# A hybrid decoder trunk on one core: up products of the recurrent stage as three single-pass products, merged products kept in used-up input rows, and the first weight tile loaded by quarters

## The chip, the cores and the metric

The kernel runs on one core of a Trainium2 chip. The metric is the device time of one execution in microseconds. The kernel before was run three times: 2075.19, 2076.61 and 2077.98 us, median 2076.61 us. The profile comes from one more execution of 2077.07 us.

## The reference, cut to what matters

One inference step of a decoder layer on 288 token columns: 256 of a prompt, 32 of eight short sequences. `D_MODEL` is 2048. All weights and inputs are float32.

```python
xn = rmsnorm(x, g_mix)
u  = xn @ w_in                 # columns: RWKV | mLSTM | pooling | three merge gates of 2048
o_rw   = rwkv7_mix(u_rw, ...)  # delta-rule recurrence, 16 heads x 64
o_ml   = mlstm_mix(u_ml, ...)
o_pool = pool_mix(u_pool, ...)
g = split(u_gate, 3)
merged = sigmoid(g0)*(o_rw@w_up_rwkv) + sigmoid(g1)*(o_ml@w_up_mlstm) + sigmoid(g2)*(o_pool@w_up_pool)
x = x + merged @ w_out
# then cross-attention into 256 memory tokens, a hierarchical mixture of experts, final RMSNorm
```

The change touches the input projection's first tile, the products `o_ml @ w_up_mlstm` and `o_pool @ w_up_pool` (here called the up products), and where `merged` lies.

## The kernel before, in words

All matrices are kept with features on the 128 partitions and tokens (T = 288) along the free axis. The program runs five blocks one after the other, each with its own instruction order per engine and semaphores between engines: `stage_front` (the input projection, mLSTM, pooling), `stage_rwkv` (the recurrent stage), `stage_merge`, `stage_cross`, `stage_moe`. Instructions on an engine run in the order written; `Steps` is a helper that gives each named step a semaphore count, and `q`, `v`, `a`, `g_` are those counters of TensorE, VectorE, ScalarE and GpSimd.

Most large products use split operands. A float32 tile w is rounded into `high` (by ScalarE, a copy into type fp32r), the remainder w - high is written as `rest` (by VectorE, over the raw weights), and the same is done for the activations. The product is then three fp32r matmuls: high by x_high, high by x_low, rest by x_high. In the trace these are single matmuls; a plain float32 matmul appears as two records.

**Front.** `stage_front` takes 58 tiles of 128 output columns from `w_main`, three slots deep (`weights(t)`, L303). Tile 0 waits for the activations: ScalarE makes `x_high` from 16 rows (L579), then `w_high` of tile 0 (`split`, L537); VectorE makes `x_rest` (L765), then `w_rest` (`rest`, L643); TensorE pairs high and low passes (L375, L376) and ends with the rest passes (L380). GpSimd squares and adds the 16 rows for the RMS norm meanwhile (L821 to L826).

**Recurrent stage.** `stage_rwkv` has a loop of N = 8 iterations. Each handles two heads of the recurrence, a long chain of small products and elementwise steps, and fills TensorE's waits with pieces of large products: `filler(name, lo, hi)`. The fills of an iteration are four gate tiles G00, G01, G10, G11 (16 row blocks of x, split, 48 passes each) and four up tiles U00, U01, U10, U11 (8 row blocks of `o_ml` or `o_pool`, plain float32, 8 products each, L1088). In a name the first digit is which of two output tiles, the second is 0 for mLSTM and 1 for pooling. One iteration on TensorE runs: U00, first half of U01, the small products z, a (L1120, L1121) and ss (L1123), G00, rest of U01, G01, transposes, small products; then seven levels l = 0 to 6 of a block inverse, each with products z (L1168), t (L1189) and u (L1192); fills stand between z and t and behind u: G10 at level 1, U10 at level 2 in two halves, U11 at levels 4 and 5 in quarters. Then the output part with G11 in pieces, and the group norm: products mean (L1286), bonus, var (L1290).

The edge between two iterations is a chain: var (TensorE), ve (VectorE L1561), groot (ScalarE L1372, square root), a reciprocal and three more steps on VectorE up to o (L1568), then z of the next iteration, which waits for o. ScalarE after groot runs `split("00")` (L1309), then kksq (L1318, which waits for o), then tz and ta (L1320, L1322). VectorE goes on with dx_v, us_v, half of `rest("00")` (L1420), sg (L1435), a, cs and so on to ssm, the other half of `rest("00")`, a reciprocal, kk (L1454). ScalarE does `split("01")` when G00's high passes are through, then the exponentials from kk (ek, L1327).

Before the loop ScalarE and GpSimd copy the 16 rows of `x_rest` from the place where `mrg` will lie into `ring` and `x_low_end`, since the merged products are written over it; after the loop they copy them on to `o_ml`'s place for `stage_merge` (L1299, L1375, L1580, L1610).

Of the kernel before, what the change touches and what calls it, by code (L numbers as in the profile page):

```python
# [126 lines left out]
def program(nc, A, O):  # L127
    with ExitStack() as ctx:
# [40 lines left out]
        with ExitStack() as mix:  # L169
# [5 lines left out]
            x_new = rounded("x_rest_late", [P, KD, T], "o_ml")  # L175
# [16 lines left out]
def stage_front(nc, ctx0, A, O, env):  # L192
# [9 lines left out]
    with ExitStack() as ctx:  # L202
# [29 lines left out]
        square, dn = placed("square", [P, T], "front", 10272), placed("dn", [P, T], "front", 10272)  # L232
# [13 lines left out]
        slot = [sem(f"f_slot{s}") for s in range(SLOTS)]  # L246
        squares, rooted, summed, variance, inverse = (sem(f"f_{n}") for n in "squares rooted summed var inverse".split())
# [53 lines left out]
        def _(sp):  # L301
# [61 lines left out]
        def _(pe):  # L363
            mm, ident = nc.tensor.matmul, K("ident")

            def tile(t):
                pe.wait_ge(w_high, t + 1)
# [117 lines left out]
            for t in range(O0):  # L485
# [3 lines left out]
                if t == SUM_AFTER:  # L489
                    pe.wait_ge(constants_in, 16)  # L490
                    pe.wait_ge(squares, 2 * KD - 1)
# [35 lines left out]
        def _(act):  # L527
# [48 lines left out]
            for k in range(KD):  # L576
                if k % 4 == 0:
                    act.wait_ge(x_in[k // 4], 16)
                fn(x_h[:, k, :], x[:, k, :], ACT.Copy, scale=par("g_mix", k)).then_inc(x_high, 1)  # L579
            for t in range(-1, O0):  # L580
# [57 lines left out]
        def _(dve):  # L638
# [128 lines left out]
            for t in range(SUM_AFTER + 2):  # L767
                rest(t)
            dve.wait_ge(summed, 1)
# [43 lines left out]
        def _(pool):  # L813
# [3 lines left out]
            for k in range(KD):  # L817
                if k % 4 == 0:
                    pool.wait_ge(x_in[k // 4], 16)
                if k == 0:  # L820
                    tt(rstd[:, :], x[:, k, :], x[:, k, :], ALU.mult).then_inc(squares, 1)  # L821
                    continue
                pool.wait_ge(squares, 2 * k - 1)
                tt(square[:, :], x[:, k, :], x[:, k, :], ALU.mult).then_inc(squares, 1)
                pool.wait_ge(squares, 2 * k)
                tt(rstd[:, :], rstd[:, :], square[:, :], ALU.add).then_inc(squares, 1)  # L826
# [79 lines left out]
def stage_rwkv(nc, ctx0, A, O, env):  # L906
# [11 lines left out]
    with ExitStack() as ctx:  # L918
# [21 lines left out]
        env["sb"]("x_low_end", [P, T], ctx)  # L940
# [5 lines left out]
        x_h, x_old, x_new = env["x_h"], env["x_l"], env["x_new"]  # L946
        x_l, x_le = rounded("rx_low", [P, KD - 1, T], "ring", 8192), rounded("rx_low_end", [P, T], "x_low_end")
        low = lambda k: x_l[:, k, :] if k < KD - 1 else x_le[:, :]
# [12 lines left out]
        xl_in, xl_out = sem("w_xlin"), sem("w_xlout")  # L961
# [3 lines left out]
        pe_steps = ["U00", "z", "a", "ss", "H00", "G00", "U01", "H01", "G01", "tr0", "tr1", "tr2"]  # L965
        pe_steps += [f"bk{x}{h}" for x in H for h in H] + ["sk0", "sk1", "w0", "w1"]
        fill_after = {1: ["G10"], 2: ["U10"], 5: ["U11"]}
        for l in LV:
            pe_steps += [f"z{l}"] + ([] if l == 0 else (["H10"] if l == 1 else []) + [f"t{l}", f"u{l}"] if l < 6 else [f"u{l}"])
# [6 lines left out]
        dve_steps = ["dx_v", "us_v", "sg", "a", "cs", "cen", "csc", "csm", "ssm", "l00",  # L976
                     "rec", "kk", "kap", "rt", "b", "bt", "l01", "ka", "kp", "kt", "rkk", "s00", "m00", "s01", "m01"]
        dve_steps += [f"bk{x}{h}" for x in H for h in H] + ["sk0", "sk1", "wm0", "w0", "wm1", "w1"]
        for l in LV:
            dve_steps += (["l10"] if l == 1 else []) + ([f"u{l}", f"t{l}"] if l == 0 else [f"t{l}", f"u{l}"] if l < 6 else [f"u{l}"])  # L980
            if l < 2:
                dve_steps += ["su0", "st0"] if l == 0 else ["su1"]
# [4 lines left out]
            if l == 5:  # L987
                dve_steps += ["l11"]
        dve_steps += ["s0", "s1a", "s1", "ds", "dsp", "ysum", "s11", "d", "m11", "ve", "grec", "y", "bon", "o"]
# [1901 lines left out]
```

## Time and profile before

| | us |
|---|---|
| median of 3 runs | 2076.61 |
| profiled execution | 2077.07 |
| its span | 2075.3 |
| TensorE busy in the span | 1850.8 (89%) |
| VectorE busy | 943.3 (45%) |
| ScalarE busy | 596.6 (29%) |
| GpSimd busy | 394.6 (19%) |
| recurrent stage, first up product to the last iteration's end | about 484 to 1169 |

The span runs from the first to the last recorded instruction. A timeline row gives start, duration, engine, line, operation, output and inputs, how many instructions were merged into it, and in brackets how long the engine was idle before it and what released it. A TensorE duration contains the pipeline's latency, so the distance between starts is the price of an instruction in a row of equal ones. L numbers are lines of the kernel above.

### The profile page before, as it was taken

The numbers are of one execution on the slowest core, as the hardware profiler recorded it, in microseconds if no ns is written. First come the engines' busy times: TensorE is split into PE (matmuls) and PEld (weight loads), VectorE is DVE, ScalarE is ACT, GpSimd is POOL, SyncE is SP. The second block draws the span as 40 slices with busy tenths as digits, with TensorE's granted clock in tenths as the row PEclk, the third lists the DMA queues.
The fourth block names the chain that finished last, engine by engine and source line by source line (L and its number), as shares of the span: only waits on it lengthen the run. The fifth ranks groups of instructions, "written<-read, shape, count | busy, mean of one in ns | idle before, by whom it ended". The sixth has DMA issues, their size and how long they took to land. (4 is left out here: it accounts for less than half of the span.)

```text
span 2075.3 us, 33706 instructions
## 1 busy us (share of the span) xinstructions
PE 1850.8 (89%) x13379; PEld 1552.9 (75%) x13379; DVE 943.3 (45%) x1521; ACT 596.6 (29%) x838; POOL 394.6 (19%) x362
## 2 busy tenths in 40 slices
PE   6999999998999999999999899999988878767765
PEld 6999999997777777878778799999977534443432
DVE  5553444546474564654646454555543111112213
ACT  3343223323133232332332433334444111100112
POOL 7550003112220311203212000184023000000002
PEclk9999999999999999999999899999998988898888
DMA  6444344434132222221221444643672999999996
GB/s 254 163 162 174 122 165 165 141 121 139 50 111 78 69 93 73 91 83 61 98 78 51 142 169 182 242 163 135 235 313 82 410 430 432 431 432 431 431 431 259
DMA packets 46168, 409.33 MB, mean 197 GB/s; under 512 B 6532, under 2 KB 8328, under 8 KB 16136
## 3 DMA queue, kind: packets, MB, share of 16 engines
q1 hardware_dynamic: 46088, 408.17, 50.9%
q8 instruction: 61, 1.00, 0.2%
q14 instruction: 19, 0.16, 0.0%
HBM read 396.98 MB, written 11.18 MB: 197 GB/s over the span
## 5 line engine op out<-in xcount | busy, mean ns | idle before, releaser
L375 PE MATMUL ps<-x_high,w_high 128*128 128x288 f32 x928 | 255.7, 302 | 15.8 <-ACT w_high L537 15.4
L376 PE MATMUL ps<-x_rest,w_high 128*128 128x288 f32 x928 | 251.7, 298 | 0.0
L375 PEld LDWEIGHTS ps<-x_high,w_high 128*128 128x128 f32 x928 | 176.3, 190 | 18.7 <-ACT w_high L537 15.9
L376 PEld LDWEIGHTS ps<-x_rest,w_high 128*128 128x128 f32 x928 | 176.1, 190 | 0.5
L537 ACT ACTIVATE w_high<-w_raw 128x2048 fp32r<-128x2048 f32 x58 | 111.0, 1915 | 164.6 <-DMA w_raw<-in_w_main 88.3
L643 DVE TENSOR_TENSOR w_rest<-w_raw,w_high 128x2048 fp32r<-128x2048 f32 x58 | 139.2, 2402 | 23.2 <-ACT w_high L537 23.1
L1105 PE MATMUL ps<-x_high,r_high 128*128 128x288 f32 x512 | 145.5, 309 | 0.0
L380 PE MATMUL ps<-x_high,w_rest 128*128 128x288 f32 x928 | 133.0, 296 | 2.2 <-DVE w_rest L643 2.2
L1590 POOL TENSOR_TENSOR xm<-ring,const 128x512 f32<-128x512 f32 x56 | 72.3, 1291 | 324.8 <-DVE ring L1487 231.9
L1105 PE MATMUL ps<-rx_low,r_high 128*128 128x288 f32 x480 | 130.9, 299 | 0.0
L380 PEld LDWEIGHTS ps<-x_high,w_rest 128*128 128x128 f32 x928 | 126.8, 189 | 2.4 <-DVE w_rest L643 2.4
L2435 PE MATMUL ps<-half_a,xg 128*32 128x512 f32 x256 | 72.8, 721 | 58.6 <-DMA half_b<-in_w_egu 58.3
L1105 PEld LDWEIGHTS ps<-x_high,r_high 128*128 128x128 f32 x512 | 96.4, 188 | 8.8 <-DVE sk L1491 6.7
L2556 POOL TENSOR_SCALAR fin<-xn,param 128x288 f32<-128x288 f32 x12 | 11.8, 1003 | 465.6 <-DVE xn L2775 465.6
L2418 PEld LDWEIGHTS ps<-put,x2t 128*128 128x128 f32 x768 | 89.0, 195 | 14.4 <-issue 14.4
L1830 ACT ACTIVATE gw_high<-ring 128x2048 fp32r<-128x2048 f32 x46 | 87.6, 1904 | 41.1 <-PE ps L1785 27.8
L2579 ACT ACTIVATE xg<-ps 128x512 f32<-128x512 f32 x32 | 19.1, 597 | 270.2 <-PE ps L2418 270.2
L2737 DVE TENSOR_TENSOR xn<-xn,ps 128x288 f32<-128x288 f32 x112 | 42.0, 446 | 113.5 <-PE ps L2412 113.5
L2435 PEld LDWEIGHTS ps<-half_a,xg 128*32 128x32 f32 x256 | 18.7, 129 | 100.0 <-issue 99.4
L2418 PE MATMUL ps<-put,x2t 128*128 128x128 f32 x768 | 92.8, 280 | 0.4 <-PEq L121 0.4
L1105 PEld LDWEIGHTS ps<-rx_low,r_high 128*128 128x128 f32 x480 | 90.4, 188 | 1.4
L1342 ACT ACTIVATE ring<-ps 128x512 f32<-128x512 f32 x48 | 28.7, 597 | 198.1 <-PE ps L1168 198.1
(570 smaller groups left out, 4317.1 us busy)
## 6 DMA issues: line engine op xcount, KB each, us to landing
w_raw<-in_w_main SPq DMA_DIRECT2D x58, 1024.0 KB, 4.9
ring<-in_w_g SPq DMA_DIRECT2D x32, 1024.0 KB, 4.9
half_a<-in_w_egu SPq DMA_DIRECT2D x16, 2048.0 KB, 18.6
half_b<-in_w_egu SPq DMA_DIRECT2D x16, 2048.0 KB, 23.0
ring<-in_w_u SPq DMA_DIRECT2D x32, 512.0 KB, 3.5
ring<-in_w_gate SPq DMA_DIRECT2D x8, 2048.0 KB, 8.0
ring<-in_w_out SPq DMA_DIRECT2D x8, 2048.0 KB, 8.1
half_d<-in_w_egu SPq DMA_DIRECT2D x8, 2048.0 KB, 22.4
```

Of the source, the lines that this page charges most:

```text
L375: mm(o, high[:, t % 2, k, :], x_h[:, k, :], start=(k == 0), stop=False)
L376: ins = mm(o, high[:, t % 2, k, :], x_l[:, k, :], start=False, stop=False)
L380: ins = mm(o, w_rest[:, t % SLOTS, k, :], x_h[:, k, :], start=False, stop=(k == KD - 1))
L537: fn(high[:, t % 2, :, :], raw[:, t % SLOTS, :, :], ACT.Copy).then_inc(w_high, 1)
L643: tt(w_rest[:, t % SLOTS, :, :], raw[:, t % SLOTS, :, :], high[:, t % 2, :, :], ALU.subtract).then_inc(w_low, 1)
L1105: ins = mm(o, high[:, k, :], low(k) if t % 2 else x_h[:, k, :], start=(t == 0), stop=False)
L1342: a.done(fn(zm, ps[:, 6, :].rearrange("p (j t) -> p j t", j=4), ACT.Copy), f"z{l}")
L1590: g_.done(tt(xm[:, l % 2, :, :], bb, K(f"level{LEVELS[l]}").unsqueeze(1).to_broadcast([P, 4, P]), ALU.mult), f"x{l}")
L1830: copy = lambda out, src: nc.scalar.activation(out, src, ACT.Copy)
L2418: ins = mm(ps[:, g % 2, (k % 4) * P:(k % 4 + 1) * P], x2t[:, c, k * P:(k + 1) * P], put[:, c, :], start=(c == 0), stop=(c == C - 1))
L2435: ins = mm(ps[u * CAP:(u + 1) * CAP, 2, :], xg[:, 4 * g + k, u * CAP:(u + 1) * CAP], w[u // 2][:, u % 2, k, :], start=(g == k == 0), stop= ...
L2737: v.done(tt(res[:, k, :], res[:, k, :], ps[:, BANKS[k % len(BANKS)], 0:T], ALU.add), f"s{k}")
```

## The change

In the front: the first weight tile is loaded as four quarters, each behind a quarter of x, and ScalarE converts each quarter between the quarters of x. TensorE's tile 0 waits for the quarter that it needs. The squares for the norm move from GpSimd to one ScalarE instruction over all 16 rows (behind tile 2's conversion), and their sum to one VectorE reduction (behind tile 2's rest).

In the recurrent stage: the up products become three fp32r passes each (24 passes a tile instead of 8 float32 products). `o_ml` and `o_pool` are split before the loop: 16 high copies on ScalarE, 8 remainders on VectorE and 8 on GpSimd. Each up tile gets `split_up` on ScalarE (128x1024 into one `u_high` buffer, so the next split waits for the last tile's high passes, step V) and `rest_up` on VectorE (over the raw weights, step n). The merged products go to rows 8 to 23 of `rwx`, the RWKV input rows that an iteration has used up, so x_rest stays where it is, and the copies of it before and behind the loop go. The first gate weights of `stage_merge` wait for one more step (n00). `stage_merge` reads the merged products from their new place.

```diff
@@ stage_front, sync
-                sp.dma_start(x[:, 4 * n:4 * n + 4, :], A["xT"][:, 4 * n:4 * n + 4, :]).then_inc(x_in[n], 16)
-            for t in range(SLOTS):
+                k = slice(4 * n, 4 * n + 4)
+                sp.dma_start(x[:, k, :], A["xT"][:, k, :]).then_inc(x_in[n], 16)
+                sp.dma_start(raw[:, 0, k, :].rearrange("p k n -> p (k n)"), A["w_main"][0, :, 512 * n:512 * n + 512]).then_inc(first_w[n], 16)
+            for t in range(1, SLOTS):
                 weights(t)
@@ stage_front, tensor, tile(t)
                     if t == 0:
+                        pe.wait_ge(*((first_high, k // 4 + 1) if k < 12 else (w_high, 1)))
                         pe.wait_ge(x_high, k + 1)
                         pe.wait_ge(x_rest, k + 1)
@@ stage_front, scalar
+            for n in range(4):
+                act.wait_ge(x_in[n], 16)
+                for k in range(4 * n, 4 * n + 4):
+                    fn(x_h[:, k, :], x[:, k, :], ACT.Copy, scale=par("g_mix", k)).then_inc(x_high, 1)
+                act.wait_ge(first_w[n], 16)
+                fn(high[:, 0, 4 * n:4 * n + 4, :], raw[:, 0, 4 * n:4 * n + 4, :], ACT.Copy).then_inc(w_high if n == 3 else first_high, 1)
+            for t in range(O0):
                 split(t + 1)
+                if t == 1:
+                    act.wait_ge(x_rest, KD)
+                    fn(x[:, :, :], x[:, :, :], ACT.Square).then_inc(squares, 1)
@@ stage_front, vector
             for t in range(SUM_AFTER + 2):
                 rest(t)
+                if t == 2:
+                    dve.wait_ge(squares, 1)
+                    nc.vector.tensor_reduce(rstd[:, :], x[:, :, :].rearrange("p k t -> p t k"), AX.X, ALU.add).then_inc(squares, 1)
@@ stage_rwkv, sync, behind the last iteration's loads
             load_own(N - 1)
+            sp.wait_ge(q.sem, q.at("U10", N - 1))
+            load_up("00", N - 1)
             sp.wait_ge(q.sem, q.at("H11", N - 1))
+            sp.wait_ge(v.sem, v.at("n00", N - 1))
             sp.dma_start(ring[:, GATE_SLOT[0], :], A["w_gate"][0, :, :]).then_inc(env["merge_slots"][GATE_SLOT[0]], 16)
...
-            sp.wait_ge(xl_out, KD)
             sp.dma_start(ring[:, UP_SLOT[0], 0:2048], A["w_up_rw"][0, :, :]).then_inc(env["merge_slots"][UP_SLOT[0]], 16)
@@ stage_rwkv, tensor
+            pe.wait_ge(ml_rest, KH)
...
+                        lap = i - 1 if name == "U00" else i
                         if lo == 0:
-                            pe.wait_ge(up_slots[b], i * 32 + 16 * d + 16)
+                            pe.wait_ge(a.sem, a.at("k" + name[1:], lap))
+                            if name == "U00":
+                                pe.wait_ge(first_high, 1)
+                            elif name == "U01":
+                                pe.wait_ge(pool_rest, KH)
                             pe.wait_ge(v.sem, v.at(f"m1{b}", i - 1) if d == 0 else v.at(f"m0{b}", i))
+                        o = ps[:, (1, 7)[b], 0:T]
                         for t in range(lo, hi):
-                            src = (o_ml, o_pool)[b]
-                            ins = mm(ps[:, (1, 7)[b], 0:T], w_up[:, b, t, :], src[:, t, :], start=(t == 0), stop=(t == KH - 1))
+                            k = t // 2 if t < 2 * KH else t - 2 * KH
+                            if t < 2 * KH:
+                                ins = mm(o, u_high[:, k, :], o_l[b][:, k, :] if t % 2 else oh(b, k), start=(t == 0), stop=False)
+                                if t == 2 * KH - 1:
+                                    q.done(ins, "V" + name[1:])
+                                continue
+                            if k == 0:
+                                pe.wait_ge(v.sem, v.at("n" + name[1:], lap))
+                                if name == "U00":
+                                    pe.wait_ge(first_rest, 1)
+                            ins = mm(o, u_rest[:, b, k, :], oh(b, k), start=False, stop=(k == KH - 1))
...
-                filler("U00", 0, 8)
-                filler("U01", 0, 4)
+                filler("U00", 0, 24)
+                filler("U01", 0, 12)
...
-                    name, *parts = {1: ("G10", 18, 32, 48), 2: ("U10", 0, 4, 8), 4: ("U11", 0, 2, 4), 5: ("U11", 4, 6, 8)
+                    name, *parts = {1: ("G10", 18, 32, 48), 2: ("U10", 0, 12, 24), 4: ("U11", 0, 6, 12), 5: ("U11", 12, 18, 24)
@@ stage_rwkv, scalar: before the loop, and the new step's places
+            for k in range(KH):
+                fn(oh(0, k), o_ml[:, k, :], ACT.Copy).then_inc(o_high, 1)
+            act.wait_ge(up_slots[0], 16)
+            fn(u_high[:, :, :], w_up[:, 0, :, :], ACT.Copy).then_inc(first_high, 1)
...
-            for k in range(0, KD, 2):
-                fn(low(k), x_old[:, k, :], ACT.Copy).then_inc(xl_in, 1)
+            for k in range(KH):
+                fn(oh(1, k), o_pool[:, k, :], ACT.Copy).then_inc(o_high, 1)
...
+                def split_up(name):
+                    n = order.index(name)
+                    lap = i + 1 if n == 0 else i
+                    act.wait_ge(up_slots[n % 2], lap * 32 + 16 * (n // 2) + 16)
+                    act.wait_ge(q.sem, q.at("V" + order[n - 1], i))
+                    act.wait_ge(v.sem, v.at("n" + order[n - 1], i - 1 if n == 1 else i))
+                    if n == 1:
+                        act.wait_ge(first_rest, 1)
+                    a.done(fn(u_high[:, :, :], w_up[:, n % 2, :, :], ACT.Copy), "k" + name)
...
                 split("00")
+                split_up("01")
                 act.wait_ge(v.sem, v.at("o", i - 1))
                 a.done(fn(ekap, kk, ACT.Square), "kksq")
...
                 split("10")
+                split_up("10")
...                                       # level 3
                         split("11", 8, 16)
+                        split_up("11")
...                                       # behind sa1
+                split_up("00")
@@ stage_rwkv, vector: before the loop, and the new step's places
+            for j in range(KH):
+                dve.wait_ge(o_high, j + 1)
+                tt(o_l[0][:, j, :], o_ml[:, j, :], oh(0, j), ALU.subtract).then_inc(ml_rest, 1)
+            dve.wait_ge(first_high, 1)
+            tt(u_rest[:, 0, :, :], w_up[:, 0, :, :], u_high[:, :, :], ALU.subtract).then_inc(first_rest, 1)
...
+                def rest_up(name):
+                    WA("k" + name)
+                    b = int(name[1])
+                    v.done(tt(u_rest[:, b, :, :], w_up[:, b, :, :], u_high[:, :, :], ALU.subtract), "n" + name)
...
                 rest("00", 8, 16)
+                rest_up("01")
                 WA("root")
...                                       # level 1, behind su1
+                        rest_up("10")
...
                     if l == 4:
+                        rest_up("11")
+                    if l == 5:
                         rest("11", 0, 8)
-                    if l == 5:
+                    if l == 6:
                         rest("11", 8, 16)
...                                       # behind dsp
+                rest_up("00")
                 WA("ys")
@@ stage_rwkv, gpsimd
-            for k in range(1, KD, 2):
-                nc.gpsimd.tensor_copy(low(k), x_old[:, k, :]).then_inc(xl_in, 1)
+            for j in range(KH):
+                pool.wait_ge(o_high, KH + j + 1)
+                tt(o_l[1][:, j, :], o_pool[:, j, :], oh(1, j), ALU.subtract).then_inc(pool_rest, 1)
```

## Rows read from the trace of the kernel before

**Rows 1.** Stage windows: one iteration; busy time, granted clock, DMA share, GB/s.
```profile
741.03:825.46 84.43, 78.35 (x554) 65.95 (x554) 47.76 (x80) 25.16 (x43) 17.34 (x14) 1.00 0.25 84
```

**Rows 2.** Timeline, TensorE, start of iteration 3 (start, duration, engine, line).
```profile
741.03 4.12 PE L1088 MATMUL ps<-o_ml,ring 128*128 128x288 f32 x16
...
747.02 0.51 PE L1120 MATMUL ps<-rwx,wa 64*128 64x288 f32 x1
...
748.43 0.29 PE L1105 MATMUL ps<-rx_low,r_high 128*128 128x288 f32 x1
...
752.44 0.29 PE L1105 MATMUL ps<-rx_low_end,r_high 128*128 128x288 f32 x1
```

**Rows 3.** Timeline, ScalarE, the same stretch.
```profile
743.48 1.91 ACT L1309 ACTIVATE r_high<-ring 128x2048 fp32r<-128x2048 f32 x1
745.93 0.44 ACT L1318 ACTIVATE f<-f 128x288 f32<-128x288 f32 x1 [0.54 <-DVE rwx L1568]
...
752.85 1.92 ACT L1309 ACTIVATE r_high<-ring 128x2048 fp32r<-128x2048 f32 x1 [0.98 <-PE ps L1105]
...
756.08 0.44 ACT L1327 ACTIVATE f<-f 128x288 f32<-128x288 f32 x1
```

**Rows 4.** Timeline, VectorE, the same stretch.
```profile
745.38 0.52 DVE L1568 SCALAR_TENSOR_TENSOR rwx<-f,param 128x288 f32 x1 [0.19 <-DVE f L1566]
...
751.30 1.22 DVE L1420 TENSOR_TENSOR r_rest<-ring,r_high 128x1024 fp32r<-128x1024 f32 x1
...
754.42 0.46 DVE L1454 TENSOR_TENSOR f<-f 128x288 f32<-128x288 f32 x1
```

**Rows 5.** Timeline, TensorE, levels 2 and 3 of that iteration.
```profile
786.65 1.06 PE L1192 MATMUL ps<-ring 128*128 128x128 f32 x8
...
789.49 1.05 PE L1168 MATMUL ps<-ring,xm 128*128 128x128 f32 x8
791.38 1.16 PE L1189 MATMUL ps<-ring 128*128 128x128 f32 x8 [0.84 <-ACT ring L1342]
```

**Rows 6.** Timeline, TensorE, level 1 of the next iteration, around 16 single passes.
```profile
863.11 1.06 PE L1192 MATMUL ps<-ring 128*128 128x128 f32 x8
...
866.22 0.31 PE L1201 MATMUL ps<-st_,sxm 32*32 32x32 f32 x4
```

**Rows 7.** Timeline, VectorE, end of iteration 3 (dsp and ysum).
```profile
821.59 0.69 DVE L1552 TENSOR_TENSOR sts<-sts,f 128x512 f32<-128x512 f32 x1
822.85 0.19 DVE L1554 TENSOR_TENSOR f<-f 128x32 f32<-128x32 f32 x1 [0.56 <-ACT f L1367]
```

**Rows 8.** Timeline, TensorE, end of iteration 3 (mean).
```profile
823.10 0.75 PE L1286 MATMUL ps<-f,const 128*128 128x288 f32 x2 [0.50 <-DVE f L1554]
```

**Rows 9.** Timeline, TensorE, start of the recurrent stage.
```profile
484.24 6.80 PE L1088 MATMUL ps<-o_ml,ring 128*128 128x288 f32 x16 [7.38 <-DVEq L1408]
...
492.90 0.51 PE L1120 MATMUL ps<-rwx,wa 64*128 64x288 f32 x1
```

**Rows 10.** Timeline, ScalarE, start of the recurrent stage: eight copies.
```profile
481.20 2.76 ACT L1299 ACTIVATE rx_low<-x_rest 128x288 fp32r<-128x288 f32 x8
```

**Rows 11.** Timeline, VectorE, start of the merge: eight remainders of that shape.
```profile
1173.66 3.03 DVE L1941 TENSOR_TENSOR gr_rest<-rwx,gr_high 128x288 fp32r<-128x288 f32 x8
```

**Rows 12.** DMA issues on the page: KB each, median us to landing.
```profile
ring<-in_w_gate SPq DMA_DIRECT2D x8, 2048.0 KB, 8.0
```

**Rows 13.** Timeline, ScalarE, start of the front.
```profile
6.65 6.92 ACT L579 ACTIVATE x_high<-x_in,param 128x288 fp32r<-128x288 f32 x16
```

**Rows 14.** Timeline, VectorE, start of the front.
```profile
7.30 14.17 DVE L765 SCALAR_TENSOR_TENSOR x_rest<-x_in,param,x_high 128x288 fp32r<-128x288 f32 x16 [7.30 <-ACT x_high L579]
```

**Rows 15.** Timeline, TensorE, rest passes of tiles 0 and 1.
```profile
24.32 3.32 PE L380 MATMUL ps<-x_high,w_rest 128*128 128x288 f32 x16 [2.21 <-DVE w_rest L643]
...
32.33 2.30 PE L380 MATMUL ps<-x_high,w_rest 128*128 128x288 f32 x16
```

**Rows 16.** Stage windows behind TensorE's wait of 2.21 us (granted clock third from last).
```profile
26.00:28.00 2.00, 2.00 (x10) 2.00 (x10) 2.00 (x2) 0.27 (x1) 1.92 (x2) 0.50 0.00 0
```

More of the change, by code:

```diff
@@ L231, in stage_front @@
         rstd = env["rstd"]
-        square, dn = placed("square", [P, T], "front", 10272), placed("dn", [P, T], "front", 10272)
+        dn = placed("dn", [P, T], "front", 10272)
         gt, nout = placed("gt", [P, 24], "front", 10560), placed("nout", [P, MLH, 9], "front", 10584)
@@ L246, in stage_front @@
         slot = [sem(f"f_slot{s}") for s in range(SLOTS)]
+        first_w, first_high = [sem(f"f_first{n}") for n in range(3)] + [slot[0]], sem("f_firsth")
         squares, rooted, summed, variance, inverse = (sem(f"f_{n}") for n in "squares rooted summed var inverse".split())
@@ L960, in stage_rwkv @@
         gate_slots, up_slots = env["gate_slots"], env["up_slots"]
-        xl_in, xl_out = sem("w_xlin"), sem("w_xlout")
+        o_high, ml_rest, pool_rest, first_high, first_rest = (sem(f"w_{n}") for n in ("ohigh", "mlrest", "poolrest", "firsth", "firstr"))
         wa_in, st_in, st_out, stp_out = sem("w_wa"), sem("w_stin"), sem("w_stout"), sem("w_stp")
         LV = range(len(LEVELS))
-        pe_steps = ["U00", "z", "a", "ss", "H00", "G00", "U01", "H01", "G01", "tr0", "tr1", "tr2"]
+        pe_steps = ["V00", "U00", "z", "a", "ss", "H00", "G00", "V01", "U01", "H01", "G01", "tr0", "tr1", "tr2"]
         pe_steps += [f"bk{x}{h}" for x in H for h in H] + ["sk0", "sk1", "w0", "w1"]
-        fill_after = {1: ["G10"], 2: ["U10"], 5: ["U11"]}
+        fill_after = {1: ["G10"], 2: ["V10", "U10"], 5: ["U11"]}
         for l in LV:
-            pe_steps += [f"z{l}"] + ([] if l == 0 else (["H10"] if l == 1 else []) + [f"t{l}", f"u{l}"] if l < 6 else [f"u{l}"])
+            pe_steps += [f"z{l}"] + ([] if l == 0 else (["H10"] if l == 1 else ["V11"] if l == 5 else []) + [f"t{l}", f"u{l}"] if l < 6 else [f"u{l}"])
             if l in fill_after:
@@ L986, in stage_rwkv @@
                 dve_steps += ["m10"]
-            if l == 5:
-                dve_steps += ["l11"]
-        dve_steps += ["s0", "s1a", "s1", "ds", "dsp", "ysum", "s11", "d", "m11", "ve", "grec", "y", "bon", "o"]
+            if l == 4:
+                dve_steps += ["n11"]
+        dve_steps += ["l11", "s0", "s1a", "s1", "ds", "dsp", "n00", "ysum", "s11", "d", "m11", "ve", "grec", "y", "bon", "o"]
         v = Steps(ctx, nc, "w_dve", dve_steps)
-        act_steps = ["h00", "kksq", "tz", "ta", "root", "h01", "ek", "er", "ekap", "ec", "G00", "G01", "tr0", "tr1", "tr2", "h10"]
+        act_steps = ["h00", "k01", "kksq", "tz", "ta", "root", "h01", "ek", "er", "ekap", "ec", "G00", "G01", "tr0", "tr1", "tr2", "h10", "k10"]
         for l in LV:
@@ L994, in stage_rwkv @@
             if l == 3:
[L995 to L996 removed]
+                act_steps += ["G10", "h11", "k11"]
+        act_steps += ["g0", "gs", "sa0", "sas", "g1", "sa1", "k00", "ys", "G11", "sq", "groot"]
         a = Steps(ctx, nc, "w_act", act_steps)
@@ L1372, in _ @@
                 a.done(fn(ek, ek, ACT.Sqrt), "groot")
-            act.wait_ge(q.sem, q.at("U11", N - 1))
-            for k in range(0, 10):
-                fn(x_new[:, k, :], low(k), ACT.Copy).then_inc(xl_out, 1)
         @block.vector
@@ L1605, in _ @@
                 pool.wait_ge(v.sem, v.at("m11", i))
-                m = mrg[:, bass.ds(i * 2 + 1, 1), :].rearrange("p o t -> p (o t)")
+                m = rwx[:, bass.ds(i + 2 * KH, 1), 0:T].rearrange("p o t -> p (o t)")
                 g_.done(tt(m, m, gtmp[:, :], ALU.add), "m1")
-            pool.wait_ge(q.sem, q.at("U11", N - 1))
-            for k in range(10, KD):
-                nc.gpsimd.tensor_copy(x_new[:, k, :], low(k)).then_inc(xl_out, 1)
 def of_own_seq(x):
@@ L1871, in _ @@
                     act.wait_ge(v.sem, v.at("m3", k // 4))
-                copy(m_h[:, k, :], mrg[:, k, :]).then_inc(mh, 1)
+                copy(m_h[:, k, :], merged(k)).then_inc(mh, 1)
             for j in range(TILES):
```

65 lines of the change are left out of this document (24 added, 41 removed).

## The prediction

> **What bounds the kernel now.** I read the stage windows first: in an iteration of the recurrent stage, 84.43 us long, TensorE is busy for 78.35 us [rows 1], so products look like the thing to shorten. But that share says nothing of order, so I then read each engine's timeline over the edge between two iterations and over one level. At the edge the reader is to see three engines that finish together. TensorE passes the time from var to z with up products [rows 2], z being the first step that needs o. ScalarE runs the conversion for G00 until 745.39 and then waits 0.54 us for VectorE's o [rows 3], which ends at 745.90 [rows 4]. So the up products there are cover for a chain, and a shorter cover ends the iteration earlier only as far as o and ScalarE let it: to 745.95 instead of 747.02. In the levels the fills stand between z and t, where without a fill TensorE waits 0.84 us for ScalarE's copy [rows 5], and behind u, where they are pure TensorE time. In the front TensorE starts its first rest passes at 24.32 after a wait of 2.21 us for VectorE [rows 15]; before them lie ScalarE's 16 row conversions and VectorE's 14.17 us of remainders [rows 13, 14]. These are the places to price.
>
> **Price of a product.** U00 and half of U01 are 12 float32 products in 747.02 - 741.03 = 5.99 us, 0.499 us each [rows 2]. 30 single passes took 752.44 - 748.43 = 4.01 us, 0.134 us each, so three cost 0.401 us. On TensorE the change saves 0.098 us on each of 8 x 32 = 256 products, 25 us. How much of it moves the end is the question.
>
> **Edge between iterations (7 times).** U00 now needs 24 x 0.134 = 3.2 us: 741.03 to 744.3. U01's first half then waits for k01, its conversion on ScalarE, which stands behind the conversion for G00. That ends at 743.48 + 1.91 = 745.39 [rows 3]; a 128x1024 piece of the same conversion costs between half (0.96) and all of 1.91 us; I take 1.0, since half the columns are copied, so k01 is done at 746.4. TensorE waits 2.1 us, runs 12 passes in 1.6 us and reaches z at 748.0 instead of 747.02: +1.0. Behind the waiting product in TensorE's queue stand z, a and ss, and for z wait tz, sg and the whole chain to kk. kksq slips to 746.4 too, but ss comes behind z and hides it. On VectorE a new remainder (1.22 us for 128x1024 [rows 4]) stands before the reciprocal and kk: kk at 754.42 + 1.0 + 1.22 = 756.6, done at 757.1. That is hidden: ek cannot start before ScalarE has converted G01's weights and switched functions, 756.08 + 1.0 = 757.08 [rows 3]. Were that cover gone, it would cost up to 1.22 us. The rest of U01 saves 0.39 us before G01, but G01's rest passes then wait for VectorE, which is 1.0 us late. Edge: +1.0. Were k01 early enough, z would start at 745.95, -1.05; with the upper price of a conversion, +1.9.
>
> **Levels (8 times).** Sixteen passes behind a u cost 866.22 - 863.11 = 3.11 us from u to the next product [rows 6]; less 16 x 0.134 that leaves 0.97, so 12 passes make 2.57. The four float32 products there took 789.49 - 786.65 = 2.84 [rows 5]: -0.27. I put the same for the half of U10 before t. At level 3 VectorE, which works through the next iteration's mixing, comes late by what it does not gain; I take back 0.17. U11's four quarters: behind u 0.1 each (six passes for two products: 0.2 less, minus half of it for changing between kinds of product); before t almost nothing, since the way without a fill takes 791.38 - 789.49 = 1.89 us and ends on ScalarE [rows 5]; 0.03 each. Sum -0.27 - 0.27 + 0.17 - 0.26 = -0.63 an iteration. Bounds: 0, if VectorE's late remainders for U10 and U11 eat it, and 10 fewer passes' worth, 16 x 0.098 = -1.6.
>
> **End of an iteration (8 times).** The remainder for the next U00 stands between dsp and ysum on VectorE: dsp ends at 822.28, the remainder at 823.5, ysum, which ran at 822.85 behind ScalarE's copy, at 823.5 [rows 7]. mean already waited for ysum by 0.50 us [rows 8], so var and o slip with it: +0.55, between 0 (ysum late anyway) and 1.22. Its conversion k00 lies on ScalarE's long wait before ysum and is free.
>
> An iteration thus comes out at +1.0 - 0.63 + 0.55 = +0.9; the TensorE time saved mostly turns into waiting.
>
> **Start of the stage (once).** TensorE's first product waits for VectorE to come to its loop (484.24, idle 7.38 [rows 9]). VectorE now first makes eight remainders (3.03 [rows 11]) and the first up remainder (1.22): 4.25 later, 488.5. ScalarE's eight copies for them, 2.76 us by [rows 10], run beside. The first 12 products took 8.66 us here against 5.99 later: 2.67 us of half clock [rows 2, 9], so about 5.3 us at it, 20 passes of 0.267. U00 then ends at 488.5 + 5.35 + 0.5 = 494.4, z starts at 496.0 against 492.90: +3.1. Between 0 (another wait hides it) and +4.25. GpSimd's eight remainders of `o_pool` have from about 485 to 494, so they may cost 1.1 us each without being seen. The copies that fall away ran while VectorE finished o, at the end, and beside VectorE's mixing, at the start: nothing.
>
> **Merge.** Its first gate weights are now asked for when n00 is done, 823.5 in iteration 3's place, and o ends 745.90 + 84.43 + 0.55 = 830.9: 7.4 us for a load that took 8.0 [rows 12], less the change of block. +0.5, between 0 and +2, if the second load behind it slows it. The new places of the merged products change addresses, not instructions: 0.
>
> **Front.** ScalarE's work for tile 0 grows from 6.92 us by four quarters of 1.91, with their starts about 2.0: 6.65 + 6.92 + 2.0 = 15.6 [rows 3, 13]. The question is VectorE. With GpSimd squaring beside it a remainder took 14.17 / 16 = 0.89 us [rows 14]; the same operation on this shape later, with GpSimd idle, 0.52 [rows 4]. At 0.52 VectorE keeps up with ScalarE, ends at 15.7, makes tile 0's rest (two of 1.22) by 18.1, and the rest passes start at 18.2 instead of 24.32: -6.1. If the remainders keep their 0.89 us, they end at 21.5 as before: 0. I take -6.1, as the 0.52 is the same operation. The Trainium skill ("GPSIMD Engine Reference", Specifications) says that GpSimd shares its SBUF interfaces with VectorE and that instructions with two SBUF inputs contend; by it the 14.17 us shrink, and without it the front gains nothing. The trace agrees as far as 0.89 against 0.52 goes. The square and the reduction stand in queues that run ahead of TensorE by then: the rest of tile 3 is needed at about 18.2 + 3 x 6.4 = 37.4 (a tile is 48 passes); the two may take 12 us before it shows.
>
> **Sum.** +3.1 + 7 x 1.0 + 8 x (0.55 - 0.63) + 0.5 - 6.1 = +3.9. Against the profiled execution of 2077.07 us, 0.46 above the median, that is 2081.0; on the median 2080.5. To it comes the clock.
>
> **The clock.** After the wait of 2.21 us in the front the granted clock fell to 0.50, the lower of its two levels (1.2 GHz) [rows 15, 16]; tile 1's rest passes came 8.01 us behind tile 0's instead of 6.4: 1.6 us. The new wait at each edge is of 2.1 us, with busy TensorE on both sides. In its own sentence: the Trainium skill ("TensorE: Matmul & The Clock Gate", What's actually happening) says that the throttled state is the default and sustained activity releases it, which speaks against any change that turns products into waits. I put one drop in seven edges, +1.6, into the forecast: 2082.
>
> **Rivals.** *The clock falls at most edges.* 7 x 1.6 = 11.2 instead of 1.6: 2092. For it: the wait is as long as the front's. Against: products before and behind it are dense. *The conversion is not last, and the kernel is faster.* If k01 is done when U00 ends, the edges give -1.05 instead of +1.0: 7 x 2.05 = 14.4 less, 2066. Place: ScalarE between groot and kksq; it decides from k01 at 744.3, 2.1 us earlier than I find it. For: the order before had 0.54 us of slack there. Against: 1.91 us stand before it and nothing lets them start earlier. *It comes out even.* The start costs 1.5 instead of 3.1, the ysum delay is covered in part (0.2), no clock drop: 2082 - 1.6 - 1.6 - 2.8 = 2076. For: VectorE and ScalarE wait at many places. *The front's gain fails* (remainders at 0.89): 2082 + 6.1 = 2088.
>
> **How the numbers follow.** Forecast 0.44 (own range 2079 to 2086), clock at most edges 0.12, faster by the early conversion 0.13, even 0.22, front's gain fails 0.09. A measurement of this kernel can tell 0.2%, 4.2 us, from no change: faster is under 2072.4, slower over 2080.8. Faster: 0.13 and the lower tail of "even", 0.18. Same: the rest of "even" and the forecast's lower edge, 0.27. Slower: 0.55. The range of 2070 to 2090 leaves out the far ends of both first rivals and takes in the bounds of the once-paid terms.
>
> **What would show it.** In the profile after: TensorE idle some 2 us before o_pool's first up pass at each edge, released by ScalarE's up conversion; z 7.0 us behind U00's start instead of 5.99; mean released by ysum with over 1 us idle; first up product of the stage near 482 (484.24 - 6.1 + 4.25); first rest passes near 18. The prediction is wrong if that edge wait is under 1 us, if an iteration is shorter than 84.43 us, or if x_rest still takes 14 us.

## The result: slower by 0.64%, and the profile after

The changed kernel takes 2090.4 us (median of four, 2086.8 to 2091.9) against 2076.4 before (2075.2 to 2078.0), a ratio of 1.0064 with an interval of 1.0052 to 1.0077. Forecast were 2082 with a range of 2070 to 2090: the direction came out, the size was 14.0 instead of 5.6, and the time lies just beyond the range. The same kernel, run once more as e10, took 2088.8 (2085.6 to 2092.2), so the edge of the range lies within its scatter.

First the head of the page (busy time of each engine, its share of the span, instructions).

```profile
span 2089.0 us, 34430 instructions
...
PE 1835.1 (88%) x13635; PEld 1559.9 (75%) x13635; DVE 987.6 (47%) x1563; ACT 631.9 (30%) x873; POOL 363.3 (17%) x325
```

TensorE is busy for 16 us less than before (1850.8) and the span is 13.7 longer (2075.3). The stage window of one iteration, from U00 to the next U00, shows where that happens (columns as in [rows 1]: stretch, length, busy time of PE, PEld, DVE, ACT and POOL, granted clock, DMA share, GB/s).

```profile
741.16:826.97 85.81, 76.32 (x586) 66.85 (x586) 52.33 (x84) 28.92 (x47) 16.92 (x14) 1.00 0.25 81
```

Against [rows 1] TensorE does 2.03 us less and the iteration lasts 1.38 us longer: 3.41 us more of waiting in each. The edge, on TensorE, answers to [rows 2].

```profile
741.16 0.40 PE L1102 MATMUL ps<-o_high,r_up_high 128*128 128x288 f32 x1
...
743.41 1.22 PE L1110 MATMUL ps<-o_high,r_up_rest 128*128 128x288 f32 x8
746.62 0.40 PE L1102 MATMUL ps<-o_high,r_up_high 128*128 128x288 f32 x1 [1.99 <-DVE dx L1477]
...
748.42 0.51 PE L1141 MATMUL ps<-rwx,wa 64*128 64x288 f32 x1
```

U00 takes 3.5 us instead of 4.1 (both with the pipeline's latency), then TensorE stands still for 1.99, and z (748.42) is 7.26 behind U00's start instead of 5.99. The releaser named, VectorE's dx, is no input of an up product. It ended at 746.53, 0.04 us beside the one that counts, on ScalarE (compare [rows 3]):

```profile
743.63 1.91 ACT L1334 ACTIVATE r_high<-ring 128x2048 fp32r<-128x2048 f32 x1
745.45 1.04 ACT L1347 ACTIVATE r_up_high<-ring 128x1024 fp32r<-128x1024 f32 x1
```

k01 stands behind the conversion for G00 and ends at 746.49. The end of an iteration, VectorE (compare [rows 7]) and TensorE (compare [rows 8]):

```profile
822.55 0.69 DVE L1601 TENSOR_TENSOR sts<-sts,f 128x512 f32<-128x512 f32 x1
823.16 1.22 DVE L1469 TENSOR_TENSOR r_up_rest<-ring,r_up_high 128x1024 fp32r<-128x1024 f32 x1
824.29 0.18 DVE L1604 TENSOR_TENSOR f<-f 128x32 f32<-128x32 f32 x1
```

```profile
824.53 0.75 PE L1307 MATMUL ps<-f,const 128*128 128x288 f32 x2 [0.99 <-DVE f L1604]
```

The remainder n00 between dsp and ysum holds mean back by 0.99 us instead of 0.50. In the levels there is a wait that before did not have, at level 4:

```profile
794.62 1.16 PE L1189 MATMUL ps<-ring,xm 128*128 128x128 f32 x8 [0.52 <-DVE ring L1567]
```

It waits for VectorE, which was held up by a mixing step:

```profile
791.43 1.53 DVE L1578 TENSOR_TENSOR dx<-rwx 128x296 f32 x1
```

The front (VectorE, then TensorE) answers to [rows 14] and [rows 15]:

```profile
7.21 1.80 DVE L774 SCALAR_TENSOR_TENSOR x_rest<-x_in,param,x_high 128x288 fp32r<-128x288 f32 x4 [7.21 <-ACT x_high L583]
```

```profile
17.93 2.39 PE L384 MATMUL ps<-x_high,w_rest 128*128 128x288 f32 x16 [1.00 <-DVE w_rest L652]
24.42 2.30 PE L384 MATMUL ps<-x_high,w_rest 128*128 128x288 f32 x16
```

The rest passes start at 17.93 instead of 24.32, and tile 1's follow 6.49 us later instead of 8.01: the clock no longer falls there. The start of the stage on TensorE (compare [rows 9]):

```profile
482.50 0.61 PE L1102 MATMUL ps<-o_high,r_up_high 128*128 128x288 f32 x1 [13.56 <-DVEq L1450]
```

GpSimd's remainders of `o_pool` run meanwhile:

```profile
477.10 5.94 POOL L1631 TENSOR_TENSOR o_pool_rest<-o_pool,o_high 128x288 fp32r<-128x288 f32 x7 [13.56 <-ACT o_high L1324]
```

And the start of the merge, SyncE's queue and ScalarE:

```profile
1170.96 0.33 SPq L1072 DMA_DIRECT2D ring<-in_w_gate  x1
1171.39 0.37 SPq L1048 DMA_DIRECT2D out_rw_p<-st  x1
1171.87 0.37 SPq L1051 DMA_DIRECT2D out_rw_s<-sts  x1
1172.29 0.52 SPq L1075 DMA_DIRECT2D ring<-in_w_gate  x1
...
1180.55 0.33 SPq L1788 DMA_DIRECT2D ring<-in_w_up_rw  x1
```

```profile
1180.65 1.91 ACT L1880 ACTIVATE gw_high<-ring 128x2048 fp32r<-128x2048 f32 x1 [6.12 <-PEq L920]
```

The last o starts at 1177.75 and ends half a microsecond later, but the block is left only at 1180.55; before, the first conversion of the merge came 1.08 us behind o's start, now 2.90. In before SyncE asked for the same load 14.9 us ahead of the last o (1168.43), not 6.8, because there was no n00 to wait for:

```profile
1153.57 0.33 SPq L1065 DMA_DIRECT2D ring<-in_w_gate  x1
...
1160.20 0.35 SPq L1047 DMA_DIRECT2D out_rw_s<-sts  x1
```

**Where the 13.7 us come from.** From the starts of o and tz in the eight iterations (o to tz is the edge, tz to g0 up to the end of the levels, g0 to o the end):

| stretch | forecast | measured |
|---|---|---|
| front (last evacuation 476.90, now 468.97) | -6.1 | -7.9 |
| start of the stage (evacuation to first tz: 16.89, now 21.29) | +3.1 | +4.4 |
| seven edges (o to tz: 2.52, now 3.87) | +7.0 | +9.4 |
| eight times the levels (tz to g0: 57.91, now 57.48) | -5.0 | -3.4 |
| eight ends (g0 to o: 24.00, now 24.47) | +4.4 | +3.8 |
| clock in the iterations | +1.6 | +3.1 |
| start of the merge, to its 15th conversion | +0.5 | +2.6 |
| behind that | 0 | +1.8 |
| sum | +5.5 | +13.8 |

The clock: the seven periods from o to o come in two kinds, four of 85.82 to 85.87 us and three of 87.38 to 87.40. In the long ones the clock falls behind the edge's wait, as in these windows at the first edge (TensorE waits until 573.39):

```profile
570.00:574.00 4.00, 2.05 (x15) 1.83 (x15) 3.34 (x7) 3.59 (x4) 0.00 (x0) 1.00 0.35 102
574.00:578.00 4.00, 4.00 (x17) 2.85 (x16) 1.37 (x3) 0.64 (x2) 0.00 (x0) 0.57 0.12 47
578.00:582.00 4.00, 4.00 (x32) 4.00 (x31) 3.81 (x10) 1.98 (x3) 0.00 (x0) 1.00 0.00 0
```

A granted clock of 0.57 over four microseconds is mostly the lower level, 1.2 GHz. Each such edge costs 1.54 us; before had two dearer iterations of 0.77. Of the 1.8 us behind the start of the merge 1.55 lie between two of its conversions that were 116.06 us apart (1329.92 and 1445.98) and now are 117.61 (1341.85 and 1459.46). That is the clock too. TensorE waits 1.50 us at this place in both kernels; behind it the granted clock stayed at 1.00 before and fell to the lower level now. First before, then the changed kernel, each time the wait and a window behind it:

```profile
1328.38 0.37 PE L1784 MATMUL ps<-gm_high,gw_high 128*128 128x288 f32 x1 [1.50 <-ACT gm_high L1830]
1330.00:1334.00 4.00, 4.00 (x23) 3.21 (x23) 4.00 (x12) 1.82 (x2) 0.00 (x0) 1.00 1.04 446
```

```profile
1340.33 0.37 PE L1834 MATMUL ps<-gm_high,gw_high 128*128 128x288 f32 x1 [1.50 <-ACT gm_high L1880]
1342.00:1346.00 4.00, 4.00 (x19) 3.93 (x19) 4.00 (x12) 1.75 (x1) 0.00 (x0) 0.57 1.02 438
```

The same wait stands in the profiles of all eleven runs, and the clock fell behind it in five (the changed kernel, e2, e5, e7 and e10). What decides it no run shows, so these 1.55 us are not shown to be a cost of the change.

### The profile page after: what moved, and what is told of

Its sections match the earlier page's. It is cut to its first block and busy times, and to the rows that moved or that the text cites. A ratio compares the mean times of both kernels' runs of the same rounds, so it can differ in the third digit from the quotient of the medians.

```text
span 2089.0 us, 34430 instructions
## 1 busy us (share of the span) xinstructions
PE 1835.1 (88%) x13635; PEld 1559.9 (75%) x13635; DVE 987.6 (47%) x1563; ACT 631.9 (30%) x873; POOL 363.3 (17%) x325
## 5 line engine op out<-in xcount | busy, mean ns | idle before, releaser
L652 DVE TENSOR_TENSOR w_rest<-w_raw,w_high 128x2048 fp32r<-128x2048 f32 x58 | 138.7, 2394 | 11.7 <-ACT w_high L541 11.6
L1126 PE MATMUL ps<-x_rest,r_high 128*128 128x288 f32 x512 | 139.6, 298 | 0.0
L1126 PEld LDWEIGHTS ps<-x_rest,r_high 128*128 128x128 f32 x512 | 96.5, 188 | 1.1
L1102 PE MATMUL ps<-o_high,r_up_high 128*128 128x288 f32 x240 | 72.8, 324 | 27.7 <-DVE dx L1477 13.8
```

Of the source, the lines that this page charges most:

```text
L652: tt(w_rest[:, t % SLOTS, :, :], raw[:, t % SLOTS, :, :], high[:, t % 2, :, :], ALU.subtract).then_inc(w_low, 1)
L1102: ins = mm(o, u_high[:, k, :], o_l[b][:, k, :] if t % 2 else oh(b, k), start=(t == 0), stop=False)
L1126: ins = mm(o, high[:, k, :], x_l[:, k, :] if t % 2 else x_h[:, k, :], start=(t == 0), stop=False)
```

## Experiments

All numbers in the table are read from the starts in each kernel's profiled execution as above; "period" is the common distance from o to o, without clock drops. Ratios are to the kernel before, run beside each.

| kernel | evacuation | to first tz | period | o to tz | o to merge | us | ratio, interval |
|---|---|---|---|---|---|---|---|
| before | 476.90 | 16.89 | 84.43 | 2.52 | 1.08 | 2076.4 | 1 |
| changed | 468.97 | 21.29 | 85.85 | 3.87 | 2.90 | 2090.4 | 1.0064, 1.0052 to 1.0077 |
| e1 front only | 469.21 | 16.64 | 84.52 | 2.52 | 1.09 | 2071.3 | 0.9972, 0.9961 to 0.9983 |
| e2 k01 first | 469.19 | 22.72 | 85.44 | 3.44 | 2.40 | 2084.7 | 1.0036, 1.0023 to 1.0049 |
| e3 n00 early | 469.39 | 21.78 | 85.36 | 3.87 | 0.89 | 2080.4 | 1.0016, 1.0007 to 1.0025 |
| e4 stores first | 469.25 | 22.14 | 85.84 | 3.86 | 0.89 | 2087.5 | 1.0041, 1.0029 to 1.0053 |
| e5 switch early | 470.91 | 21.26 | 84.23 | 2.17 | 2.73 | 2074.3 | 0.9987, 0.9978 to 0.9996 |
| e7 early entry | 470.74 | 19.31 | 85.83 | 3.85 | 2.50 | 2089.5 | 1.0066, 1.0052 to 1.0079 |
| e8 reordered | 470.68 | 19.53 | 83.71 | 2.16 | 0.89 | 2066.4 | 0.9945, 0.9932 to 0.9959 |
| e9 filled wait | 469.06 | 22.25 | 85.77 | 3.79 | 2.94 | 2087.2 | 1.0049, 1.0035 to 1.0063 |
| e10 changed | 469.46 | 21.77 | 85.84 | 3.86 | 2.41 | 2088.8 | 1.0060, 1.0046 to 1.0074 |

The evacuation of e5, e7 and e8 is some 1.6 us later than that of the others with the new front: in their profiles the granted clock between 195 and 202 us is 0.76 instead of 1.00. Their edits lie behind that stretch.

**e1, the front alone.** The front's hunks of the change in the kernel before; recurrent stage and merge untouched.

> The kernel before with only the front of the change (quarters of tile 0's weights, one Square on ScalarE, one reduction on VectorE, GpSimd's squares gone); the recurrent stage and the merge are those of before. Theory (the parts add up): the front's 7.9 us, read at the last tile's evacuation (476.90 before, 468.97 after), stay until the end: 2076.4 - 7.9 = 2068.5. Rival (the stage start takes it back, because TensorE has less to do while VectorE mixes, or a later load is not early enough): 2072 to 2076.

Measured: 2071.3, 6.0 under before; the interval of the ratio, 3.5 to 8.1 us, holds the 7.9 expected, though the median lies between the theory and its rival. In the profile, the fastest of the seven executions (2068.6), the evacuation is 7.7 us earlier and the last o 8.4 (1160.03 instead of 1168.43), and the stage's start is no longer than before. So nothing takes the front's gain back in that execution (whether the median loses up to 2 us of it is open), and the recurrent stage with the start of the merge loses 19 us (2090.4 against 2071.3).

**e2, k01 first.**

```
-                split("00")
-                split_up("01")
+                split_up("01")
+                split("00")
```

> The changed kernel with one swap on ScalarE: k01 (the conversion of U01's weights) ahead of the conversion for G00. No work is added or removed. Theory (the edge is a wait on the order of ScalarE's queue): TensorE's wait of 1.99 us ahead of U01 goes; what is then late is VectorE, whose remainder for G00 ends where it ended before, so an edge comes out about even with before instead of +1.27: 7 x 1.27 = 8.9 less; with the wait the three clock drops of 1.55 us at edges go too, 4.6: 2090.4 - 13.5 = 2076.9, and without them 2081.5. Rival (the stage is longer because VectorE has 44 us and ScalarE 35 us more to do; order does not matter): 2090.

Measured: 2084.7. The edge fell by 0.43 us, a third of what was expected. ScalarE, then TensorE:

```profile
743.43 1.28 ACT L1347 ACT_TABLE_LOAD   x1 [1.51 <-PE ps L1102]
744.72 1.06 ACT L1347 ACTIVATE r_up_high<-ring 128x1024 fp32r<-128x1024 f32 x1
```

```profile
745.90 0.40 PE L1102 MATMUL ps<-o_high,r_up_high 128*128 128x288 f32 x1 [1.58 <-ACT r_up_high L1347]
```

Here the releaser is ScalarE by name: it was k01 that U01 waited for. But k01 first has its own wait. There is one buffer for the up weights' high part, V00 reads it until 743.4, and the function switch away from Sqrt (1.28 us), which in the changed kernel ran ahead of the conversion for G00, now comes behind that wait. The queue's order alone brought a third of what it promised; the one buffer and the switch held back the rest.

**e5, the switch early.** The swap of e2, and ahead of k01 `fn(spare[:, 0:8], param[:, 0:8], ACT.Copy)`, a copy of 128x8.

> The swap of e2 and one tiny copy (128x8) ahead of k01, so that ScalarE's function switch from Sqrt to Copy (1.28 us) runs while it would wait for TensorE to have read the single high buffer (V00) to its end. In e2 that wait ended at 743.43, the switch came behind it, and U01 waited 1.58 us. Theory (two layers: first the queue order, then buffer and switch): k01 runs 743.4 to 744.5, U01 starts at 744.6 instead of 745.9, an edge is 1.3 to 1.5 us shorter than in the changed kernel and the clock does not fall there: 2090.4 - 7 x 1.4 - 4.6 = 2076. Rival (VectorE, which waits 0.61 us for G00's high part in e2, and not the up conversion, sets the edge now): as e2, 2084.7.

Measured: 2074.3, 10 us under e2 and just under before. ScalarE, then TensorE:

```profile
739.49 1.28 ACT L1352 ACT_TABLE_LOAD   x1
740.78 0.21 ACT L1352 ACTIVATE spare<-param 128x8 f32<-128x8 f32 x1
741.01 1.06 ACT L1347 ACTIVATE r_up_high<-ring 128x1024 fp32r<-128x1024 f32 x1
```

```profile
742.20 0.40 PE L1102 MATMUL ps<-o_high,r_up_high 128*128 128x288 f32 x1 [0.30 <-DVE f L1616]
```

The wait of 1.99 us is 0.30, the edge 2.17, under the 2.52 of before. That settles the edge: 1.70 us of each come from the place of one conversion and one function switch, and no edge of this profile has a clock drop.

**e3, n00 early.**

```
+                rest_up("00")
                 WQ("ds")
 ...
-                rest_up("00")
                 WA("ys")
```

> The changed kernel with one move on VectorE: the remainder for the next U00 stands between s1 and ds instead of between dsp and ysum, in a gap of 1.36 us that VectorE spends waiting for TensorE. Theory (it delayed ysum, and with it mean, var and o): TensorE's wait ahead of mean goes from 0.99 back to 0.50 us, 8 x 0.54 = 4.3 less: 2086.1. Rival (mean waits for G11's product or for ScalarE anyway, or the remainder now delays ds): 2089 to 2091.

Measured: 2080.4, 10 us under the changed kernel instead of 4.3. VectorE, then TensorE:

```profile
732.99 1.22 DVE L1469 TENSOR_TENSOR r_up_rest<-ring,r_up_high 128x1024 fp32r<-128x1024 f32 x1
734.42 0.69 DVE L1600 TENSOR_TENSOR sts<-sts,ps 128x512 f32<-128x512 f32 x1 [0.22 <-PE ps L1302]
```

```profile
736.65 0.75 PE L1307 MATMUL ps<-f,const 128*128 128x288 f32 x2 [0.51 <-DVE f L1604]
```

The period fell by 0.49, as the theory said (8 x 0.49 = 3.9). Two effects were not in it. The merge's first load and the stores behind it wait for n00, so they too go out earlier: o to merge is 0.89, 2.0 less. And no iteration of the profile has a clock drop, though the edge's wait of 2.0 us is still in each; this is one execution, 2.4 us under the median of eleven.

**e4, the stores first.** `store(N - 1)` ahead of the wait for n00 and the gate load, on SyncE.

> The changed kernel with SyncE's last stores (out_rw_p, out_rw_s) issued ahead of the first gate load of the merge instead of behind it. Theory (the block of the recurrent stage ends only when these stores have landed, 8.3 us after their issue because 2 MB of weights are ahead of them in the queue): the block ends with o as before, ScalarE's first conversion of the merge starts at the landing of its load or at the block's end, 1.8 to 2.6 earlier: 2088.2. Rival (the gate load itself, asked for 8 us before it is needed, is what is late): no change, 2090.4.

Measured: 2087.5. Its interval touches that of the changed kernel, so the time alone does not tell them apart; in the profile o to merge is 0.89 instead of 2.90.

```profile
1168.16 0.35 SPq L1051 DMA_DIRECT2D out_rw_s<-sts  x1
1169.23 0.34 SPq L1073 DMA_DIRECT2D ring<-in_w_gate  x1
```

The gate load is issued 6.85 us ahead of o's start here, 6.79 in the changed kernel, and yet the conversion comes 2.0 us sooner. The DMA issues of the end of the block (KB, us to landing) show where they come from; first the changed kernel, then e4 (in the kernel before 8.0 and 2.1):

```profile
ring<-in_w_gate SPq DMA_DIRECT2D x1, 2048.0 KB, 8.4
out_rw_s<-sts SPq DMA_DIRECT2D x1, 256.0 KB, 8.3
```

```profile
ring<-in_w_gate SPq DMA_DIRECT2D x1, 2048.0 KB, 7.6
out_rw_s<-sts SPq DMA_DIRECT2D x1, 256.0 KB, 2.0
```

With the issue times above, the load of the changed kernel lands at 1179.4, 1.6 us behind o's start, and the stores behind it at 1180.2; the block waits for the stores and is left at 1180.55. In e4 the load lands at 1176.8, 0.7 behind o's start, and the conversion follows at 1176.97. So theory and rival each have about half: 0.9 us of the 2.0 are the load itself, which was late and here lands sooner, 1.1 the way from its landing over the stores to the next block. Before, too, the stores stood behind the load, but it had been asked for so early that it landed at 1161.6, 6.9 us ahead of the last o. That fits e3: there the load goes out 9.1 us ahead of o, the stores still land behind it (7.2 us), and o to merge is 0.89.

The Trainium skill ("DMA: Bandwidth & Descriptors", Queues, rings and completion order) says that a DMA's completion mark lands only behind every earlier write of the same DMA engine; the trace agrees, with stores that land 8.3 us after their issue and 0.8 behind the load ahead of them, against 2.0 with no load ahead in e4.

**e7, the early entry.** VectorE's `dve.sem_inc(v.sem, v.n)` moved up from behind the mixing to behind the first up remainder; ScalarE's first Square waits for the mixing itself.

> The changed kernel with VectorE's entry count of the recurrent stage (what TensorE's first up product waits for) given right behind the first up remainder instead of behind the mixing of k and r; the first Square of the stage waits for that mixing itself. Theory (the start's loss of 4.4 us is a wait for VectorE's queue): the first pass starts near 477 instead of 482.5, U01 then waits for GpSimd's remainders of o_pool (end 484.0), z at 485.8 instead of 489.4: 3.5 less, 2086.9. Rival (VectorE's mixing, slowed beside GpSimd's remainders, is behind z anyway, or the half clock eats it): 2089 to 2090.

Measured: 2089.5, no difference that can be told from the changed kernel. TensorE:

```profile
477.90 0.60 PE L1102 MATMUL ps<-o_high,r_up_high 128*128 128x288 f32 x1 [7.19 <-DVE o_ml_rest L1441]
...
486.12 0.40 PE L1102 MATMUL ps<-o_high,r_up_high 128*128 128x288 f32 x1 [2.25 <-POOL o_pool_rest L1632]
```

The wait moved. The first pass starts 7.2 us behind the evacuation instead of 13.5, runs at half clock, and then U01 waits for GpSimd's remainders of `o_pool`. 2.0 of 4.4 us come back in the profile, not in the time.

**e9 and e10, the wait filled, and the changed kernel again.** e9 puts `mm(ps[:, 7, 0:T], ident, rstd[:, :], start=True, stop=True)` three times ahead of the wait for k01; what they compute is overwritten.

> The changed kernel with three float32 products (0.5 us each) of no use put ahead of U01's first pass, into the bank that this pass overwrites, so that TensorE is idle for 0.5 us at the edge instead of 1.99; k01 and everything behind it start as before. Theory (besides its length the wait costs clock: three drops of 1.55 us at edges in the changed kernel's profile): the edge keeps its 3.87 us from o to tz, no drop stands in the iterations, 4.6 less: 2085.8. Rival (the drops have another cause, or come by chance): as the changed kernel, 2089 to 2091.

> The changed kernel itself once more, beside e9 on the same chip: 2090.4, with drops at two to three of its seven edges, by every theory.

Measured: 2087.2 and 2088.8; the intervals overlap, so the time does not tell them apart. TensorE in e9:

```profile
744.17 1.62 PE L1095 MATMUL ps<-rstd,const 128*128 128x288 f32 x6
746.25 0.40 PE L1106 MATMUL ps<-o_high,r_up_high 128*128 128x288 f32 x1 [0.47 <-ACT r_up_high L1351]
```

In the profiles e9 has no long edge (3.77 to 3.81, one iteration 0.3 longer), e10 has two long ones (4.67 and 4.76, periods of 87.41 and 87.59). That fits the clock theory in one execution each, and e9's is the fastest of its five (2084.35); as a cost in the median it is not shown.

**e8, all orders together.** e5, e3, e4, e7, and the remainder for U01 behind kk.

> The changed kernel with all the orders put right at once: k01 first with the early function switch (e5), the remainder for the next U00 in VectorE's gap (e3), the one for U01 behind kk, the last stores ahead of the merge's first load (e4), the early entry (e7). Same products and passes as the changed kernel. Theory (the passes are worth something once nothing waits for their conversions): front -7.9, start +0.9, seven edges at -0.1 to -0.9, levels -3.4, ends 0, merge 0 to +0.8: some 12 under before, 2064 (2061 to 2069), that is faster than the front alone (e1, 2071.3). Rival (what the passes save lies beside other work; at best even): 2070 to 2073, as e1.

Measured: 2066.4, ratio 0.9945, the fastest of all, and its interval lies below that of e1. Its profiled execution is the longest of its five (2074.75; the others 2064.4 to 2067.3): behind the stage, in the merge, TensorE waits 3.41 us for GpSimd's sum of squares, and one iteration has a clock drop. An iteration of it without one:

```profile
657.62:741.30 83.68, 76.42 (x586) 66.91 (x586) 52.33 (x85) 29.12 (x47) 16.89 (x13) 1.00 0.25 83
```

The same products as in the changed kernel (76.42 against 76.32 us of TensorE), 2.13 us less of an iteration. So it was the order, not the work on VectorE and ScalarE, that made the changed kernel slower, and the three passes, with the moved places that came with them, bring about 5 us of the 25 that they save on TensorE (2066.4 against e1's 2071.3) once little waits for them.

## Why the prediction was right in direction and short by 8 us

- **Edge, +1.0: right mechanism, mis-sized at +1.35.** TensorE's wait was forecast at 2.1 us and is 1.99; z behind U00 at 7.0 and is 7.26. k01 ended 5.33 us behind U00's start, forecast 5.37; but from U01's first pass to z went 1.80 us, not 1.6, and o itself came 0.08 sooner. The rival "the conversion is not last", k01 done at 744.3, was further off than the prediction said: even first in the queue (e2) k01 ended at 745.78, since the one buffer is read until 743.4 and the function switch follows. Neither stood in the prediction.
- **Levels, -0.63: -0.43.** The gain on TensorE was there; VectorE's mixing (one dx of 1.53 us, begun 0.14 behind a GpSimd operation, where another takes 0.46) came late for level 4, by 0.52 us. I had taken 0.17 for it.
- **End, +0.55: +0.47,** and e3 gives it back. Right.
- **Start, +3.1: +4.4.** First pass forecast near 482, measured 482.50, but that is luck, because the front gained more: it is 13.5 us behind the evacuation, forecast 11.6. The failed term is GpSimd's remainders of `o_pool` at no cost. Beside them the mixing of k and r took from 476.73 to 482.39, 5.7 us instead of 3.3, and with an early entry they are themselves what U01 waits for (e7). That they slow the mixing is read from the trace; no run takes them away.
- **Merge, +0.5: +2.6.** The step was right as far as it went: the load was asked for 7.3 us ahead of o's end, forecast 7.4, took 8.4 instead of 8.0 and landed 1.1 us behind o's end instead of 0.6. It left out two small stores behind the load in the same queue, whose landing the block waits for (e4): the conversion came 1.3 us behind the load's landing.
- **Front, -6.1: -7.9.** The rest passes at 18.2, measured 17.93; x_rest went from 0.89 to 0.45 each. What remains of the gain is the clock drop of [rows 16], which I had seen and not subtracted. The Trainium skill ("GPSIMD Engine Reference", Specifications) has GpSimd contend for shared SBUF interfaces with VectorE instructions that have two SBUF inputs, as these remainders do; the trace agrees, 0.89 us with GpSimd beside it and 0.45 without.
- **Clock, +1.6: +3.1 in the iterations** (three drops of 1.54 instead of one, and two of 0.77 in before gone). The rival "at most edges" had the price right (1.6) and the count too high. Each edge waits for some 1.97 us, and at three of them the clock fell.

Of the missing 8.3 us the clock has 3.0 (1.5 in the iterations, 1.5 in the merge, where the forecast had none), the edge 2.4, the start of the merge 2.1, the levels 1.6 and the start 1.3; front and ends give back 2.4, and 0.2 are not accounted for. No step had the wrong sign.

## What to carry to other kernels

When a long operation is shortened that covered a chain on other engines, list all that its helpers wait for, in the order of their queue: the queue itself, the single buffer that must be read out, the function switch behind that wait. Put a helper where its engine idles (n00) and the function switch ahead of the wait, with a tiny instruction (e5): the same products, 24 us apart between the changed kernel and e8. And at the end of a block look at what a load for the next block must now wait for before it is asked for, and at the stores that this block waits for and that stand behind it in the queue.

## What the runs showed of the hardware that was not expected

- ScalarE's function switch runs behind the wait of the instruction that it is placed at, not during it: in e2 at 743.43, after 1.51 us of idle time. It stands at the first Copy behind the square root, and no further switch stands before the Tanh at 748.58. With a copy of 128x8 ahead (0.21 us) it ran during the wait, and e5's iterations are 1.2 us shorter than e2's.
- A wait at a fixed place does not always cost clock. With 1.94 to 2.03 us at each of seven edges the clock fell at three in the changed kernel's profile, at two in that of e10, the same kernel, at two in e7's, at one in e4's and at none in e3's; behind the 1.50 us in the merge it fell in five profiles of eleven. In e3 the later wait, before mean, was down from 0.99 to 0.51; whether that is the reason no run shows.
- VectorE beside GpSimd's subtractions at the start of the stage, and the same operation on the same shape at an edge, with GpSimd idle:

```profile
477.22 0.94 DVE L1422 SCALAR_TENSOR_TENSOR f<-dx,param,rwx 128x256 f32<-128x256 f32 x1
...
746.66 0.48 DVE L1422 SCALAR_TENSOR_TENSOR f<-dx,param,rwx 128x256 f32<-128x256 f32 x1
```
